# The mixers of a two-layer hybrid block in another order: convolution before queries and keys, state sums before the attention, bias added in PSUM

## What is computed

```python
u = rms_norm(x, attn_norm_w) @ w_in
hq, hf, hi, hg, aq, ak, av, sz, sxbc, sdt = jnp.split(u, points, axis=-1)
mix = concatenate([hgrn2_mixer(hq, hf, hi, hg, ...),
                   dilated_attention_mixer(aq, ak, av, q_norm_w, k_norm_w, rel_bias),
                   mamba2_mixer(sz, sxbc, sdt, conv_w, conv_b, ...)])
x = x + mix @ w_out
x = x + peer_ffn(rms_norm(x, ffn_norm_w), ...)
# attention: s = q k^T + bias, masked; softmax; o = p v        (q, k normalized per head of 64)
# mamba2: xbc = silu(conv4(xbc) + b); cum = cumsum(dt * A)
#         y = ((C B^T) * exp(cum_t - cum_s)) (x * dt) + d_skip * x; y = rms_norm(y * silu(z))
```

## Time and profile before

| | us |
|---|---|
| median of 3 runs | 2966.87 |
| lowest, highest | 2962.67, 2971.38 |
| the profiled execution | 2973.62 |
| its span in the profile | 2971.8 |

### The profile page before, as it was taken

One profiled execution on the slowest core, in us unless ns is written; L12 is line 12 of the kernel. 1 busy time (PEld: TensorE's weight loads), 2 busy tenths in 40 slices (PEclk: granted clock), 3 DMA queues, 4 the chain that ended last, 5 costly groups with the idle time before them and its releaser, 6 DMA issues.

```text
span 2971.8 us, 43765 instructions
## 1 busy us (share of the span) xinstructions
PE 2924.6 (98%) x17198; PEld 2587.8 (87%) x17198; DVE 2022.1 (68%) x3133; ACT 1456.4 (49%) x2275; POOL 16.7 (1%) x40
## 2 busy tenths in 40 slices
PE   8999999999999999999999999999999999999998
PEld 7888888889999888888888999997898998888997
DVE  6859998765555685889885655567666556665554
ACT  6531775554444553257545444445455444545443
POOL 0000000000000000000000000000000000000000
PEclk9899999999999998999999999999999999999999
DMA  6334456774554433444668555556555656554563
GB/s 193 98 129 156 157 178 204 250 273 173 196 196 172 159 103 107 156 156 170 203 225 294 184 196 184 183 184 180 179 171 176 185 188 183 173 180 146 150 186 135
DMA packets 223293, 528.50 MB, mean 178 GB/s; under 512 B 13498, under 2 KB 87392, under 8 KB 212128
## 3 DMA queue, kind: packets, MB, share of 16 engines
q1 hardware_dynamic: 221872, 521.11, 52.9%
q0 software_dynamic: 1264, 5.25, 0.5%
HBM read 507.42 MB, written 18.88 MB: 177 GB/s over the span
## 4 chain that ended last, share of the span: by engine, by line
PE 92%; DVE 6%; ACT 1%; DMA 1%; issue 1%; SPq 0%; DVEq 0%; ACTq 0%
PE ps L2357 15%; PE ps L1275 15%; PE ps L2341 12%; PE ps L1325 12%; PE ps L1335 12%; PE ps L1309 11%; PE ps L559 3%; PE ps L568 2%; PE ps L1264 2%; PE ps L2601 1%; DVE ring_lo L542 1%; PE ps L692 1%; DVE arena L1626 1%; PE ps L1086 1%; PE ps L2524 0%
## 5 line engine op out<-in xcount | busy, mean ns | idle before, releaser
L1995 DVE TENSOR_TENSOR ring_lo<-ring,w_hi 128x1024 fp32r<-128x1024 f32 x320 | 388.7, 1224 | 264.6 <-ACT w_hi L1991 263.2
L1991 ACT ACTIVATE w_hi<-ring 128x1024 fp32r<-128x1024 f32 x320 | 336.4, 1056 | 263.5 <-PE ps L2357 178.5
L1275 PE MATMUL ps<-h_t,ring 128*128 128x256 f32 x2048 | 463.5, 379 | 0.9 <-ACT arena L908 0.9
L1275 PEld LDWEIGHTS ps<-h_t,ring 128*128 128x128 f32 x2048 | 379.2, 190 | 47.4 <-issue 1.3
L1325 PE MATMUL ps<-h_t_lo,down_hi 128*128 128x256 f32 x1024 | 288.3, 282 | 0.0
L1325 PE MATMUL ps<-h_t_expert,down_lo 128*128 128x256 f32 x1024 | 288.0, 281 | 0.0
L1325 PE MATMUL ps<-h_t_expert,down_hi 128*128 128x256 f32 x1024 | 286.9, 280 | 0.0
L2341 PE MATMUL ps<-h_t_hi,w_hi 128*128 128x256 f32 x928 | 260.2, 280 | 2.8 <-ACT arena L2147 2.7
L2341 PE MATMUL ps<-h_t_lo,w_hi 128*128 128x256 f32 x928 | 261.6, 282 | 0.0
L2341 PE MATMUL ps<-h_t_hi,ring_lo 128*128 128x256 f32 x928 | 259.8, 280 | 0.0
L1788 DVE TENSOR_TENSOR up_lo<-ring,up_hi 128x2048 fp32r<-128x2048 f32 x64 | 146.7, 2292 | 98.9 <-ACT up_hi L971 98.9
(11 more groups left out here) (463 smaller groups left out, 6682.2 us busy)
## 6 DMA issues: line engine op xcount, KB each, us to landing
ring<-in_peer_down SPq DMA_DIRECT2D x128, 1024.0 KB, 5.1
ring<-in_w_in SPq DMA_DIRECT2D x140, 512.0 KB, 3.7
ring<-in_peer_up SPq DMA_DIRECT2D x68, 1024.0 KB, 4.8
ring<-in_w SPq DMA_DIRECT2D x132, 512.0 KB, 3.7
ring<-in_peer_up SPq DMA_DIRECT2D x120, 512.0 KB, 4.2
arena<-late_gates SPq DMA_DIRECT2D x16, 1024.0 KB, 6.8
ring<-in_w_out SPq DMA_DIRECT2D x16, 512.0 KB, 3.6
ring<-in_peer_w_query SPq DMA_DIRECT2D x16, 512.0 KB, 4.3
```

What stands on the lines that cost most here:

```text
L1275: m = pe.e.matmul(PS[:, act_bank(b), j * T:(j + 1) * T], RING[:, b % 2, j * D + kc * P:j * D + (kc + 1) * P], HT[:, kc, :], start=kc == 0, ...
L1991: a.e.activation(W_HI[:, g % HI_SLOTS, :], RAW[:, g % RAW_SLOTS, :], ACT.Copy).then_inc(*a.count(f"c{g}_hi"))
L1995: v.e.tensor_tensor(RAW_LO[:, g % RAW_SLOTS, :], RAW[:, g % RAW_SLOTS, :], W_HI[:, g % HI_SLOTS, :].bitcast(F32), ALU.subtract).then_inc(* ...
```

## The change

Five things happen at once.

- Blocks change places: the convolution's input (columns 2560 and 3072 on) becomes blocks 2 and 3, the attention's become 4 and 5. The transposes, C B products and state sums (`ss_out0`, `ss_out1`) move in front of pieces (6, 0), and queries' transposes, scores and probabilities behind them. The decays get a place of their own (`DECAYS`).
- The six flip matmuls leave the front. Each score tile now is two matmuls into the same place, q k and FLIP times the raw bias; VectorE adds only the mask (its bias additions are gone).
- The first tap of the convolution goes from VectorE to ScalarE (`taps`), in seven activations.
- ScalarE also takes the squares of queries and keys (`qk_sq`), their scaling out of PSUM (`qkt`), and the copy and square of the recurrence's output (`hg_read`).
- Block 6 waits for `ss_read`, VectorE's read of the state sums, since both lie in banks 0 and 1.

Tables and helpers:

```diff
-PROB_BANKS = (4, 5, 6, 7, 2)
+PROB_BANKS = (4, 5, 6, 7, 0)
...
-    ("w_in", 0, KD, 0, 512), ("w_in", 0, KD, 512, 256), ("w_in", 0, KD, 768, 512), ("w_in", 0, KD, 1280, 512),
-    ("w_in", 0, KD, 2560, 512), ("w_in", 0, KD, 3072, 390), ("w_in", 0, KD, 1792, 512), ("w_in", 0, KD, 2304, 256),
+    ("w_in", 0, KD, 0, 512), ("w_in", 0, KD, 512, 256), ("w_in", 0, KD, 2560, 512), ("w_in", 0, KD, 3072, 390),
+    ("w_in", 0, KD, 768, 512), ("w_in", 0, KD, 1280, 512), ("w_in", 0, KD, 1792, 512), ("w_in", 0, KD, 2304, 256),
...
+        QKSQ = score_at + AT_HEADS * (T + P)
+        QKSQ = ARENA[:, QKSQ:QKSQ + 1536]
...
-        DEC = split(SCORE, "p (h s) -> p h s", h=SS_HEADS)
...
+        DEC = split(DECAYS, "p (h s) -> p h s", h=SS_HEADS)
...
-            if j in (0, 4, 5, 10, 11):
+            if j in (0, 2, 3, 10, 11):
```

ScalarE:

```diff
-            tokens_out(2)
...
-            tokens_out(3)
+
+            def taps(first, last, ready):
+
+                a.e.wait_ge(*a.at(ready))
+                for c in range(first, last):
+                    a.e.activation(XC[:, c, :], XB[:, c, 0:T], ACT.Copy, scale=hpar("conv_w", c, c + 1)) \
+                        .then_inc(*a.count(f"tap{c}"))
+
+            taps(0, 4, "h2_ev")
             front_high(a, (5, 0), (5, 1))
+            taps(4, CONV_TILES, "h3_ev")
...
+            a.e.wait_ge(*a.at("hg_out"))
+            a.e.activation(SCORE[:, 0:512], PS[:, 4, :], ACT.Copy).then_inc(*a.count())
+            a.e.activation(SCORE[:, 512:1024], PS[:, 4, :], ACT.Square).then_inc(*a.count("hg_read"))
+            tokens_out(4)
+            front_high(a, (5, 2), (5, 3))
...
+            a.e.activation(DECAYS, DECAYS, ACT.Exp).then_inc(*a.count("dec_exp"))
...
+            front_high(a, (6, 0), (6, 1))
+            tokens_out(5)
+            a.e.wait_ge(*a.mine())
+            a.e.activation(QKSQ.rearrange("p (t n) -> p t n", t=TT), U[:, :, 256:1024], ACT.Square).then_inc(*a.count("qk_sq"))
+            a.e.wait_ge(*a.at("hg_ms"))
...
-            front_high(a, (5, 2), (5, 3))
-            a.e.wait_ge(*a.at("hg_ms"))
-            a.e.activation(STAT[:, 120:128], STAT[:, 112:120], ACT.Sqrt).then_inc(*a.count("hg_sd"))
-            front_high(a, (6, 0), (6, 1), (6, 2), (6, 3))
...
+            front_high(a, (6, 2), (6, 3))
+            a.e.wait_ge(*a.at("q_scale"))
+            a.e.wait_ge(*a.at("qk_t"))
+            for c0, c1, w in ((0, 2, STAT[:, 57:58]), (2, 3, STAT[:, 57:58]), (3, 4, hpar("k_norm")), (4, 6, hpar("k_norm"))):
+                a.e.activation(QKT[:, c0:c1, :].rearrange("p c t -> p (c t)"),
+                               PS[:, 5 + c0 // 2, (c0 % 2) * T:(c0 % 2) * T + (c1 - c0) * T], ACT.Copy, scale=w) \
+                    .then_inc(*a.count("qkt" if c1 == 6 else None))
+            front_high(a, (7, 0), (7, 1))
+            tokens_out(6)
...
-            tokens_out(6)
-            a.e.wait_ge(*a.at("dec"))
-            a.e.activation(SCORE, SCORE, ACT.Exp).then_inc(*a.count("dec_exp"))
```

TensorE:

```diff
-            pe.e.wait_ge(*pe.at(f"root@in{l}"))
-            pe.e.wait_ge(*pe.at("hank_in"))
-            for h in range(AT_HEADS):
-                m = pe.e.matmul(PS[:, 4 + h // 2, (h % 2) * T:(h % 2 + 1) * T], FLIP, HANK[:, h, :], start=True,
-                                stop=True)
-            m.then_inc(*pe.count("flip"))
...
-                free = [f"h{j - 2}_ev"] + (["pt4_ev"] if j == 7 else [])
+                free = [f"h{j - 2}_ev"] + (["ss_read"] if j == 6 else [])
...
-            pe.e.wait_ge(*pe.at("bias_ev"))
+            pe.e.wait_ge(*pe.at(f"root@in{l}"))
...
             piece(4, 2)
-            pe.e.wait_ge(*pe.at("qkn"))
...
-            m.then_inc(*pe.count("qk_t"))
             piece(4, 3)
-            piece(5, 0)
-            pe.e.wait_ge(*pe.at("qkt"))
+            pe.e.wait_ge(*pe.at("dc"))
             pe.e.wait_ge(*pe.at("hg_read"))
...
-            m.then_inc(*pe.count("at_scores1"))
-            piece(5, 1)
-            piece(5, 2)
-            pe.e.wait_ge(*pe.at("at_read1"))
...
-            piece(6, 2)
-            piece(6, 3)
-            pe.e.wait_ge(*pe.at("dc"))
-            pe.e.wait_ge(*pe.at("pt4_ev"))
...
             m.then_inc(*pe.count("cum_rows"))
-            piece(7, 0)
+            piece(5, 0)
+            piece(5, 1)
             pe.e.wait_ge(*pe.at("xc6"))
-            pe.e.wait_ge(*pe.at("h6_ev"))
+            pe.e.wait_ge(*pe.at("h4_ev"))
...
+            piece(5, 2)
             pe.e.wait_ge(*pe.at("dec"))
...
             m.then_inc(*pe.count("bc"))
+            piece(5, 3)
+            pe.e.wait_ge(*pe.at("dec_bc"))
+            pe.e.wait_ge(*pe.at("xdt"))
+            for t in range(TT):
+                for h in range(SS_HEADS):
...
+                m.then_inc(*pe.count(f"ss_out{t}"))
+            piece(6, 0)
+            piece(6, 1)
+            pe.e.wait_ge(*pe.at("qkn"))
...
+            m.then_inc(*pe.count("qk_t"))
+            piece(6, 2)
+            pe.e.wait_ge(*pe.at("qkt"))
...
+            pe.e.wait_ge(*pe.at("hank_in"))
+            for h, q, k in heads():
+                to = PS[:, 4 + 2 * (h % 2) + h // 4, (h // 2 % 2) * T:(h // 2 % 2 + 1) * T]
+                pe.e.matmul(to, q[:, P:T], k, start=True, stop=False)
+                m = pe.e.matmul(to, FLIP, HANK[:, h, :], start=False, stop=True)
+            m.then_inc(*pe.count("at_scores1"))
+            piece(6, 3)
+            pe.e.wait_ge(*pe.at("at_read1"))
+            for h, q, k in heads():
+                to = PS[:, 4 + 2 * (h % 2), (h // 2) * P:(h // 2 + 1) * P]
+                pe.e.matmul(to, q[:, 0:P], k[:, 0:P], start=True, stop=False)
+                m = pe.e.matmul(to, FLIP, HANK[:, h, P:T], start=False, stop=True)
+            m.then_inc(*pe.count("at_scores0"))
+            piece(7, 0)
...
             piece(7, 1)
+            pe.e.wait_ge(*pe.at("pt4_ev"))
...
             m.then_inc(*pe.count("at_out"))
-            pe.e.wait_ge(*pe.at("dec_bc"))
-            pe.e.wait_ge(*pe.at("xdt"))
-            for t in range(TT):
-                if t:
...
-                m.then_inc(*pe.count(f"ss_out{t}"))
+            mix_turn(pe, 0, "at_mix")
             pe.e.wait_ge(*pe.at("h7_ev"))
             spin(pe, 3, 5)
-            pe.e.wait_ge(*pe.at("ss_read"))
```

VectorE:

```diff
-            v.e.wait_ge(*v.at("flip"))
-            for b in range(3):
-                v.e.tensor_tensor(BIAS1[:, 2 * b:2 * b + 2, :],
-                                  PS[:, 4 + b, :].rearrange("p (h s) -> p h s", h=2),
-                                  PHASE[:, 0:T].unsqueeze(1).broadcast_to([P, 2, T]), ALU.add).then_inc(*v.count())
-                v.e.tensor_tensor(BIAS0[:, 2 * b:2 * b + 2, :],
-                                  PS[:, 4 + b, :].rearrange("p (h s) -> p h s", h=2)[:, :, P:T],
-                                  PHASE[:, T:T + P].unsqueeze(1).broadcast_to([P, 2, P]), ALU.add) \
-                    .then_inc(*v.count("bias_ev" if b == 2 else None))
...
-                front_low(v, FRONT[FRONT.index((3, 2)) + n])
-
-            v.e.wait_ge(*v.at("h3_ev"))
-            v.e.wait_ge(*v.mine())
-            sq = SCORE[:, 0:1536].rearrange("p (t n) -> p t n", t=TT)
-            v.e.tensor_tensor(sq, U[:, :, 256:1024], U[:, :, 256:1024], ALU.mult).then_inc(*v.count())
-            v.e.wait_ge(*v.mine())
-            v.e.tensor_reduce(STAT[:, 64:88], SCORE[:, 0:1536].rearrange("p (n d) -> p n d", d=HEAD), AX.X,
-                              ALU.add).then_inc(*v.count())
-            rstd("qk", 24, HEAD, 64, 88)
...
-            front_low(v, (5, 0))
-            v.e.wait_ge(*v.at("hg_out"))
...
+
+            def conv(k, tiles, name=None):
+
+                for c in tiles:
+                    w = hpar("conv_w", k * CONV_TILES + c, k * CONV_TILES + c + 1)
+                    if k == 1:
+                        v.e.wait_ge(*v.at(f"tap{c}"))
+                    i = v.e.scalar_tensor_tensor(XC[:, c, :], XB[:, c, k:k + T], w, XC[:, c, :], ALU.mult, ALU.add)
+                    i.then_inc(*v.count(name if c == tiles[-1] else None))
+
+            def conv_step(k, tiles, name=None):
+
+                v.e.wait_ge(*v.mine())
+                conv(k, tiles, name)
+
...
+            early, late = (0, 1, 2, 3), (4, 5, 6)
+            v.e.wait_ge(*v.at("merge32"))
+            merge(0, MASKED[0])
+            front_low(v, (3, 2))
+            v.e.wait_ge(*v.at("h2_mm"))
...
+                                  ALU.mult).then_inc(*v.count("h2_ev" if b else None))
+            merge(1, MASKED[1])
+            front_low(v, (3, 3))
+            merge(2, MASKED[2])
+            front_low(v, (4, 0))
+            conv_step(1, early)
+            merge(3, MASKED[3])
+            front_low(v, (4, 1))
+            conv_step(2, early)
+            merge(4, MASKED[4])
+            front_low(v, (4, 2))
+            v.e.wait_ge(*v.at("h3_mm"))
...
+            merge(5, 0)
+            front_low(v, (4, 3))
+            conv_step(3, early)
+            conv_step(1, late)
+            front_low(v, (5, 0))
...
-            conv(3)
```

(38 more changed lines are left out.)

277 lines of the change are left out of this document (113 added, 164 removed).

## The result

The changed kernel takes 2997.44 us (median of 4 runs, 2995.36 to 3000.09), the kernel before 2969.12 on the same chip (4 runs, 2962.67 to 2974.87): a ratio of 1.0088, 95% interval 1.0072 to 1.0105: slower by 0.9%. That is +28 us where +14 was forecast, twice the size and outside the range.

The account below looks back on a forecast made before the run. TensorE, busy 2924.6 of 2971.8 us, was the bound: its work, waits and clock. Work, waits and new half speed less old gave +8.5 and +5.8 us for the layers, together +14: 2981 us, range 2964 to 2991.

Parts of the forecast that it names:

- The score groups: TensorE's products with flips at the scores: 4.9 us second tile, 2.5 first; net +2.6 us a layer after removals.
- The price of the product: At the scores, a 64-row product between full flips costs what a flip of its width does: 0.40 or 0.21 us.
- The waits: TensorE's standing over each layer's mixers: 13.6 us against 5.5 and 5.75 before, so +8.1 and +7.9.
- The clock: Half speed over the mixers: 7.5 us a layer in the change, replacing 9.7 and 12.2 lost before.
- I expect no fall there: At the decays' 6-row matmuls, which follow work without a wait, the clock was to stay up.
- The price of a stop: Half speed after the stops at (6, 0), (7, 0) and the tail: 2.4 us each, between 1.4 and 3.4.
- That the clock stays up: Rival: half speed goes at both old places, new stops cost 0.5 a layer; -1, or 2966 us; chance 0.2.
- that VectorE comes in time: Rival: VectorE reaches state sums before TensorE needs them, both long stops vanish; -11, or 2956 us; chance 0.1.
- The rival of longer half speed: Tail stays thin and falls after (6, 0) last twice as long: +26, or 2993 us; chance 0.15.
- the forecast's own dearest case: Over both layers' mixers, the highest TensorE work and clock loss together: +26 us.
- score groups near 3.9 us: Sign of error at the second tile's scores: products keep their old 0.25 us; time then 2966 or less.
- The mean clock over the stretch: Sign over the mixers: 0.93 to 0.95 granted if right, 0.98 and more if wrong.

Follow-up runs that it names:

- full rows: The changed kernel with query-key products over all 128 rows, each summing two heads, in the same order: 2988.28 us.
- both stops filled: The changed kernel with dummy matmuls, eight in front of piece (6, 0) and seven in front of (7, 0), in each layer: 2987.56 us.
- sums read first: The changed kernel with VectorE's two reads of the state sums ahead of the norm of queries and keys: 2984.45 us.
- one order: Version with flips in front, state sums behind attention's output and four low parts early, plus piece (7, 1) ahead of the probabilities' transposes: 2971.02 us.
- grouped: The changed kernel with each score group's six query-key products first, then its six flips: 2983.84 us.

## Why the prediction was wrong

**The score groups: the step that failed.** "Between full flips I let a 64-row product cost what a flip of its width does" made 4.9 and 2.5 us; measured were 7.5 and 5.0. So TensorE's work grew by 7.7 us a layer instead of 2.6, 10.2 us over both layers, which is most of the 14 that were missed. The price of the product was not the fault, as far as the runs show: in full rows the same lists take 5.2 and 2.7. What is missing is the change of rows itself, which the sum put at nothing: twelve times 0.2 us, 2.4 in each group. The prediction took its prices from two kinds that had only been seen among their own; no row showed the change from one kind to the other, and no bound held anything for it. The Trainium skill's rule on tiling modes, given above, was not weighed. The one on packing was (the Trainium skill, TensorE: Matmul & The Clock Gate, part 3); it speaks of matmuls that run side by side and backed the dearer price of a product, not a price for the change.

**The waits: right.** 1.8 at the first grams (1.6 forecast), 4.1 at (6, 0) (4.4), 3.3 at (7, 0) (3.4), 1.2 at the turn (1.3), 1.8 at (8, 0) (2.9): 12.2 us instead of 13.6. The last one was smaller only because the turn and the dummy matmuls ahead of it ran at half speed; where they ran at full, as with both stops filled or sums read first, it is 2.7. There was none between the grams and the state sums, and the first grams began 43.57 - 40.31 = 3.3 us earlier (2.8 forecast). Their releasers were the ones named.

**The clock: right in the first layer, too low in the second.** With the two corrections above the first layer comes to 8.5 + 5.1 - 1.4 = 12.2 us against the 12.3 measured, so the clock's term held. It forecast 7.5 us; by the rows it was 1.7 + 2.4 + 2.4 + 1.7 = 8.2, an estimate. What it took off for before was too small as well: 3.4 + 6.8 is 10.2 and not "9.7 in all", the figure from the rounded mean clock. The difference, 2.0 instead of 2.2, hardly moves. In the second layer the same sum gives 9.5 of 14.1. There "I expect no fall there" failed, at the decays: the six 6-row matmuls stood behind no wait and yet fell into half speed, at a granted 0.70 and 0.61 in the two slices, 3.4 us. In other kernels here the fall at this place comes in the first layer, in the second, in both or in none; why is open. The other 1.2 us of the second layer are not accounted for.

**The price of a stop: right.** 2.4 us was taken, half way between two rows; filling four of them gave 9.5, and 4.8 for two in the trace. Taking the middle of two rows was a choice and not a derivation, so some luck is in it.

**Rivals.** That the clock stays up, and that VectorE comes in time, both fell: it came 4.1 us late. The rival of longer half speed had the nearest time, 2993, for the wrong reason; the tail's falls took 1.7 us, less than before. The range ended at 2991, short of the forecast's own dearest case of 2993, although it was said to take in the bounds.

**What would show it.** The sign named for an error, score groups near 3.9 us, lay below the forecast; nothing was named above it. The mean clock over the stretch is 0.92 (0.93 to 0.95 forecast).

## What to carry to other kernels

Price a matmul by its neighbour as well as by its shape: a list of matmuls that alternates between 64 and 128 rows paid 0.2 to 0.3 us at every change here, and the same list in two groups pays it once. A unit of work that covers a wait has a worth of its own, so before it is moved, look at what stands in its old place, and which instruction of the other engine's list now stands between it and its reader. A stop of 3 to 4 us cost its length and then, at half speed, about 2.4 us more in this kernel; in one order, with 64-column matmuls behind a stop of 1.6 us, 7.5 us were lost.

## What was not expected of the hardware

- A matmul of 64 rows and 256 columns in f32 takes 0.25 us among its likes and 0.63 when it alternates with one of 128 rows and as many columns; the latter takes 0.43 and 0.63. Adding to the place in PSUM that the matmul right ahead wrote cost nothing that shows (0.43 and 0.22 with full rows; a flip that isn't right behind its product takes 0.40 in the kernel before and 0.42 grouped).
- The clock fell without any stop in front: behind six matmuls of 6 rows and 256 columns, 0.70 and 0.61 were granted in two slices, and the six took 3.41 us (2.85 in the first layer, at 1.00).
- Filling one stop need not win its fall back: behind the grams 0.66 rose to 1.00, and 0.88 and 0.78 came up 100 us later, with no gain in time. Whether the one brought the other isn't shown, and whether the fall would stay away if every thin place were dense was not tried.
